# Differential-attention row sums as two rounded products, and a regrouped output turn, in a four-layer trunk on one core

## The reference, cut to what matters

```
q, k, v = split(h @ w_in, 3)
q = rmsnorm(q.reshape(b, s, 8, 2, 64), g_qk[0])     # mean of squares over 64 columns
k = rmsnorm(k.reshape(b, s, 8, 2, 64), g_qk[1])
q, k = rope(q), rope(k)                              # latent tokens only
o = attention(q[..0], k[..0], v) - lam * attention(q[..1], k[..1], v)
out = rmsnorm(o, g_sub) * (1 - lambda_init) @ w_o
```

## Time and profile before

| | |
|---|---|
| median of 3 runs | 3439.49 us (3432.17 to 3446.27) |
| profiled execution | 3442.12 us, its span 3440.3 us |
| mean granted TensorE clock | 0.981 of full |
| PE busy | 3282.2 us (95%) |
| PEld busy | 3025.7 us (88%) |
| DVE busy | 2004.8 us (58%) |
| ACT busy | 1120.1 us (33%) |
| HBM traffic over the span | 88 GB/s |

### The profile page before, as it was taken

One profiled execution on the slowest core, in us unless ns is written; L12 is line 12 of the kernel. 1 busy time (PEld: TensorE's weight loads), 2 busy tenths in 40 slices (PEclk: granted clock), 3 DMA queues, 4 the chain that ended last, 5 costly groups with the idle time before them and its releaser, 6 DMA issues.

```text
span 3440.3 us, 53088 instructions
## 1 busy us (share of the span) xinstructions
PE 3282.2 (95%) x20608; PEld 3025.7 (88%) x20608; DVE 2004.8 (58%) x3059; ACT 1120.1 (33%) x1800; POOL 64.8 (2%) x48
## 2 busy tenths in 40 slices
PE   7899999999999998999999898999999988999999
PEld 4776689999997775999999876899999888999999
DVE  4333357777476665766854754676763888633333
ACT  3244433111145554411112444331111486311111
POOL 1211000000000000000000000000000000000000
PEclk9999999999999998999999999999999999999999
DMA  5111124455221110244532200144542221222222
GB/s 193 56 51 41 40 68 147 156 167 160 72 77 44 44 37 17 68 166 147 171 104 66 69 20 17 57 147 145 174 120 67 74 61 49 74 74 73 73 73 79
DMA packets 436802, 304.29 MB, mean 88 GB/s; under 512 B 12483, under 2 KB 414534, under 8 KB 435654
## 3 DMA queue, kind: packets, MB, share of 16 engines
q1 hardware_dynamic: 426340, 293.75, 28.2%
q10 hardware_dynamic: 10338, 8.88, 0.8%
HBM read 298.49 MB, written 4.10 MB: 88 GB/s over the span
## 4 chain that ended last, share of the span: by engine, by line
PE 85%; DVE 8%; ACT 3%; DVEq 1%; issue 1%; DMA 1%; ACTq 0%; SPq 0%
PE psA L351 29%; PE psB L351 29%; PE psD L351 7%; PE psC L414 3%; PE psA L395 3%; PE psC L367 2%; PE psB L395 2%; PE psC L406 2%; DVE work L2348 1%; PE psB L952 1%; PE psD L893 1%; PE psA L952 1%; DVE act_lo L2356 1%; DVE work L2673 1%; PE psD L925 1%
## 5 line engine op out<-in xcount | busy, mean ns | idle before, releaser
L1643 ACT ACTIVATE w_hi<-raw 128x1024 fp32r<-128x1024 f32 (+1 forms) x314 | 324.8, 1035 | 1089.8 <-PE psB L351 731.6
L2239 DVE TENSOR_TENSOR w_lo<-raw,w_hi 128x1024 fp32r<-128x1024 f32 (+1 forms) x315 | 375.8, 1194 | 314.4 <-ACT w_hi L1643 314.1
L351 PE MATMUL psA<-act_hi,w_hi 128*128 128x320 f32 x1536 | 355.7, 313 | 14.2 <-DVE w_lo L2239 14.2
L351 PE MATMUL psA<-act_hi,w_lo 128*128 128x320 f32 x1536 | 356.1, 314 | 0.0
L351 PE MATMUL psB<-act_hi,w_lo 128*128 128x320 f32 x1536 | 354.5, 312 | 0.0
L351 PE MATMUL psA<-act_lo,w_hi 128*128 128x320 f32 x1536 | 353.2, 311 | 0.0
L351 PE MATMUL psB<-act_hi,w_hi 128*128 128x320 f32 x1536 | 351.4, 310 | 0.0
L351 PE MATMUL psB<-act_lo,w_hi 128*128 128x320 f32 x1536 | 351.1, 310 | 0.0
L2269 DVE SCALAR_TENSOR_TENSOR work<-work,silu_c 128x1024 f32<-128x1024 f32 x266 | 330.0, 1282 | 12.6 <-issue 0.4
L351 PEld LDWEIGHTS psA<-act_hi,w_hi 128*128 128x128 f32 x1536 | 261.7, 191 | 16.5 <-issue 16.2
L351 PEld LDWEIGHTS psB<-act_hi,w_hi 128*128 128x128 f32 x1536 | 260.7, 189 | 0.0
(11 more groups left out here) (360 smaller groups left out, 5619.2 us busy)
## 6 DMA issues: line engine op xcount, KB each, us to landing
raw<-in_w_ffn_in SPq DMA_DIRECT2D x176, 512.0 KB, 3.8
work<-in_w_mod SPq DMA_DIRECT2D x152, 512.0 KB, 4.4
raw<-in_w_ffn_out SPq DMA_DIRECT2D x64, 512.0 KB, 4.2
raw<-in_w_ffn_out SPq DMA_DIRECT2D x32, 384.0 KB, 3.4
raw<-in_diff_w_in SPq DMA_DIRECT2D x24, 512.0 KB, 3.8
work<-in_w_mod SPq DMA_DIRECT2D x8, 1024.0 KB, 7.1
raw<-in_lru_w_in SPq DMA_DIRECT2D x16, 512.0 KB, 4.2
raw<-in_w_mod SPq DMA_DIRECT2D x12, 512.0 KB, 4.2
```

Source lines behind the costliest of these rows:

```text
L351: last = nc.tensor.matmul(out[:, b, 0:half], w[slot][:, kt * cols + c0:kt * cols + c0 + P], r[:, o:o + half], start=(kt == 0 and p == 0), ...
L1643: nc.scalar.activation(w_hi[s][:, 0:n], raw[s][:, 0:n], ACT.Copy).then_inc(hi_done, 1)
L2239: nc.vector.tensor_tensor(w_lo[s_][:, 0:n], raw[s_][:, 0:n], w_hi[s_][:, 0:n].bitcast(F32), ALU.subtract).then_inc(split_done, 1)
```

## The change

1. In differential heads, ScalarE writes the squares rounded (fp32r) into `s_hi`. VectorE then multiplies the copied query or key with itself in f32 and subtracts `s_hi`, which gives `s_lo`; both are new steps, `sqq` and `sqk`. The row sums become two products per half with a rounded block matrix, of `s_hi` and of `s_lo`. `ssq` waits for `sqq`, `ssk` for `sqk`. In VectorE's order `q_squares` stands ahead of the maximum of tile 3, `k_squares` behind `q_roped`. `s_hi` and `s_lo` are shared by query and key.
2. The output blocks are turned into psC, psD, psA, psB, psC. Six of eight tiles of the first two blocks are turned ahead of the last panel of `out3.2`, the seventh behind that panel, the eighth after the last tile. ScalarE copies and stores blocks 0, 2 and 4; VectorE copies blocks 1 and 3, and SyncE stores them.
3. `WORK` shrinks from 13312 to 13204 columns and `blocks_r` is added, filled by one VectorE copy at the start of layer 1. Some names that nothing uses are defined (left out here).

```diff
+        blocks_r = sb("blocks_r", P, F32R)[:, :]
...
-                       ["evq", "rsq", ... "v"], ["q", "qroped", "k", "kroped"])
+                       ["evq", "rsq", ... "v"], ["sqq", "q", "qroped", "sqk", "k", "kroped"])
...
+        Y_TILES = [psC, psD, psA, psB, psC]
...
+        def square_low(x_, hi, lo, tmp):
+            nc.vector.tensor_tensor(tmp, x_, x_, ALU.mult)
+            nc.vector.drain()
+            return nc.vector.tensor_tensor(lo, tmp, hi.bitcast(F32), ALU.subtract)
...
+        s_hi, s_lo = y_hi[:, 0:T], y_lo[:, 0:T]
...
# SyncE, at its end
+            for t in range(1, QT, 2):
+                sp.wait_ge(y_copied_odd, t // 2 + 1)
+                sp.dma_start(a["y_sample"][0, (t - 1) * P:t * P, :], y_tok[:, t * D:(t + 1) * D]).then_inc(y_out, 16)
...
# TensorE
+            def early_outputs():
+                for t in range(2):
+                    output_turned(t, 0, KT - 2)
...
                         pe.wait_ge(x_done, i * 2 + (base + j - 1))
+                        if j == 1 and between and isinstance(i, int):
+                            between()
...
                     def ssq(h):
-                        acts.wait(pe, "evq", h)
-                        pes.mark(sum_rows(psC, blocks, [dsq_q], TH), "ssq")
+                        dves.wait(pe, "sqq", h)
+                        pes.mark(sum_rows(psC, blocks_r, [s_hi, s_lo], TH), "ssq")
...
                     def ssk(h):
-                        acts.wait(pe, "evk", h)
-                        dves.wait(pe, "qroped", h)
-                        pes.mark(sum_rows(psC, blocks, [dsq_k], TH), "ssk")
+                        dves.wait(pe, "sqk", h)
+                        pes.mark(sum_rows(psC, blocks_r, [s_hi, s_lo], TH), "ssk")
...
+            pe.wait_ge(x_done, x_tiles[0] - 1)
+            for t in range(2):
+                output_turned(t, KT - 2, KT - 1)
             pe.wait_ge(x_done, x_tiles[0])
-            for t in range(QT):
-                if t >= 2:
-                    pe.wait_ge(y_copied, t - 1)
...
+            for t in range(2):
+                output_turned(t, KT - 1, KT).then_inc(y_turned, 1)
+            for t in range(2, QT):
+                if t == 4:
+                    pe.wait_ge(y_copied, 1)
+                output_turned(t, 0, KT).then_inc(y_turned, 1)
...
# ScalarE
-                        acts.mark(evacuate(dq_t[h.k % 2], dsq_q, psD, TH), "evq")
+                        acts.mark(evacuate(dq_t[h.k % 2], s_hi, psD, TH), "evq")
...
-            for t in range(QT):
+            for t in range(0, QT, 2):
...
# VectorE
+                    nc.vector.tensor_copy(blocks_r, blocks)
...
                         probs(h, 2)
+                        prep(q_squares)
                         largest(h, 3)
...
                         prep(q_roped)
+                        prep(k_squares)
                         largest(h, 4)
...
# VectorE, first head: q_squares at step 2 of the norm's loop, k_squares at step 7
...
+            for t in range(1, QT, 2):
+                dve.wait_ge(y_turned, t + 1)
+                nc.vector.tensor_copy(y_tok[:, t * D:(t + 1) * D].rearrange("p (b n) -> p b n", b=2),
+                                      Y_TILES[t][:, :, :]).then_inc(y_copied_odd, 1)
```

More of the change, by code:

```diff
@@ L41 @@
 SLOT = 8 * P
-WORK = 13312
+WORK = 13204
 MUNIT = 1024
@@ L293, in build @@
         y_turned, y_copied, y_out = sem("y_turned"), sem("y_copied"), sem("y_out")
+        y_copied_odd = sem("y_copied_odd")
         def steps(name, pe, act, dve, base=1):
@@ L544, in build @@
         mV = [c(6 * P), c(6 * P)]
+        sq_at = CKV_AT + 2 * NKEY
+        n_hi, n_lo = (t_[:, sq_at:sq_at + T] for t_ in (h_hi, h_lo))
+        k_hi, k_lo = (t_[:, sq_at:sq_at + NKEY] for t_ in (h_hi, h_lo))
+        r_hi, r_lo = (t_[:, sq_at + NKEY:sq_at + NKEY + T] for t_ in (h_hi, h_lo))
         m_probs = [[c(T)], [c(T)]]
@@ L974, in _, with output_turned, project @@
             x_tiles = [KT]
-            def project(name, kts, rows, last_source, plan=None, place=None, paired=False):
+            def output_turned(t, k0, k1):
+                for kt in range(k0, k1):
+                    last = nc.tensor.transpose(Y_TILES[t][:, kt // 4, (kt % 4) * P:(kt % 4 + 1) * P],
+                                               x[:, kt * T + t * P:kt * T + (t + 1) * P], ident)
+                return last
+            def early_outputs():
+                for t in range(2):
+                    output_turned(t, 0, KT - 2)
+            def project(name, kts, rows, last_source, plan=None, place=None, paired=False, between=None):
                 base = x_tiles[0]
@@ L998, in project @@
                                 last.then_inc(gemm_done, 1)
-                turns_and_mods(turn, 1 if paired else 0, KT // 2, plan, place)
+                turns_and_mods(turn, 1 if paired else 0, KT // 2 - (1 if between else 0), plan, place)
+                if between:
+                    turn(KT // 2 - 1)
                 x_tiles[0] += KT
@@ L1510, in _ @@
                     project(f"out{layer}.{ch}", size, (h_hi, h_lo), lambda: pe.wait_ge(hidden_done, base + size + 1),
-                            modulation_of(layer), ("out", ch))
-            pe.wait_ge(x_done, x_tiles[0])
-            for t in range(QT):
-                if t >= 2:
-                    pe.wait_ge(y_copied, t - 1)
[L1518 to L1522, removed]
+                            modulation_of(layer), ("out", ch),
+                            between=early_outputs if (layer, ch) == (DEPTH - 1, len(FFN_CHUNKS) - 1) else None)
+            pe.wait_ge(x_done, x_tiles[0] - 1)
+            for t in range(2):
+                output_turned(t, KT - 2, KT - 1)
+            pe.wait_ge(x_done, x_tiles[0])
+            for t in range(2):
[4 more added lines that the diff above has]
+                output_turned(t, 0, KT).then_inc(y_turned, 1)
         @block.scalar
@@ L1905, in first_query @@
                     def first_query():
-                        acts.mark(taken(2, 0, dq_t[0], dsq_q), "evq")
+                        acts.mark(taken(2, 0, dq_t[0], s_hi), "evq")
                     def first_key():
-                        acts.mark(taken(2, 1, dk_t[0][:, 0:T], dsq_k), "evk")
+                        acts.mark(taken(2, 1, dk_t[0][:, 0:T], s_hi), "evk")
                     norm(2, {0: first_query, 1: lambda: high(Head(0, 1), 0), 2: lambda: rsq(h0), 3: lambda: cached(h0),
@@ L2124, in _ @@
                     x_tiles[0] += KT
-            for t in range(QT):
+            for t in range(0, QT, 2):
                 act.wait_ge(y_turned, t + 1)
                 nc.scalar.activation(y_tok[:, t * D:(t + 1) * D].rearrange("p (b n) -> p b n", b=2),
-                                     psum[t % 2][:, :, :], ACT.Copy).then_inc(y_copied, 1)
-                act.wait_ge(y_copied, t + 1)
+                                     Y_TILES[t][:, :, :], ACT.Copy).then_inc(y_copied, 1)
+                act.wait_ge(y_copied, t // 2 + 1)
                 dst = a["y_prompt"][0] if t == 0 else a["y_sample"][0, (t - 1) * P:t * P, :]
@@ L2512, in _, with q_squares, k_squares @@
                     scale = 64 ** -0.5
+                    dve.wait_ge(const_in, 16)
+                    nc.vector.tensor_copy(blocks_r, blocks)
+                    def q_squares(h):
+                        acts.wait(dve, "evq", h)
+                        dves.mark(square_low(dq_t[h.k % 2], s_hi, s_lo, dsq_q), "sqq")
+                    def k_squares(h):
+                        acts.wait(dve, "evk", h)
+                        dves.mark(square_low(dk_t[h.k % 2][:, 0:T], s_hi, s_lo, dsq_k), "sqk")
                     def q_normed(h):
@@ L2575, in _ @@
                     h0 = Head(0, 0)
-                    norm(2, {1: lambda: rescale(2, 0, psD, first + 1, dq_t[0]), 3: lambda: low(Head(0, 1), 0),
+                    norm(2, {1: lambda: rescale(2, 0, psD, first + 1, dq_t[0]), 2: lambda: q_squares(h0), 3: lambda: low(Head(0, 1), 0),
                              4: lambda: rescale(2, 1, psA, first + 2, dk_t[0][:, 0:T]), 5: lambda: q_normed(h0),
-                             6: lambda: q_roped(h0), 8: lambda: k_normed(h0)})
+                             6: lambda: q_roped(h0), 7: lambda: k_squares(h0), 8: lambda: k_normed(h0)})
                     rescale(2, 2, psB, first + 3, dvt)
```

5 lines of the change are left out of this document (3 added, 2 removed).

## The result

| | before | after |
|---|---|---|
| median (6 executions of each) | 3439.32 us | 3459.41 us (3456.83 to 3464.7) |
| ratio, 95% interval | | 1.0058 [1.0048, 1.0068] |
| profiled execution, its span | 3442.12, 3440.3 us | 3464.7, 3462.9 us |
| mean granted TensorE clock | 0.981 | 0.976 |

The change made the kernel 20.1 us slower by the medians. The prediction said 3454 us, with 3445 to 3465 as its range. Page of the kernel after: busy time and instructions by engine, then the engines' shares of the chain that ended last, the answer to the earlier trace rows.

The account below looks back on a forecast made before the run. It took TensorE's stream plus its standstills to bound the kernel. Query -2.5, key +9.2, first head +3.7, clock +4.8 and output -0.2 gave +15.0 us; from the median 3454.5, predicted 3454 us, range 3445 to 3465.

Parts of the forecast that it names:

- rival 1: Differential heads: the clock falls in nearly every head, all seven at 1.7 to 3 us; +24, 3464 us; chance 0.17.
- Cheaper sums: Row sums on TensorE: four fp32r instructions take 0.59 us instead of 1.08, saving 0.49 us per sum, 16 sums.
- Rival 4: Row sums: the f32 sums don't get cheaper by rounding; 7.8 us more, 3462; chance 0.04.
- Query, heads 2 to 8: Query's sums: squares hidden with about 0.03 us wait, except 0.75 in the second head; sum -2.5 us.
- Key, heads 2 to 8: Key's sums: squares not hidden, TensorE stands still 2.2 us; +1.3 per head, +9.2 us for 7 heads.
- Rival 3: Key's sums: the wait is absorbed or never arises and the change gains; -10, 3430 us; chance 0.04.
- First head: First differential head: squares delay VectorE's norm, TensorE waits 3.6 us at `rotq`, about 3 at `ssk`; +3.7 us.
- Output: Output turn at the end: first store 0.6 us later, stores 6.45 instead of 7.3 us at 406 GB/s; -0.2 us.
- Clock: Differential heads: stalls lower TensorE's clock, 3 falls of 7 at 1.6 us; +4.8 us, between 0 and 21.

Follow-up runs that it names:

- e2: Kernel before plus the new output turn and only the query's sums as two rounded products, key's sums plain f32: 3444.91 us, ratio 1.0011.
- e4: Full change plus 14 unused fp32r products per head keeping TensorE busy through the stall before the key's sums: 3452.25 us, ratio 1.0035 to the kernel before.
- e5: Full change with turned tile 3 and part of the value's products moved ahead of the key's sums: 3453.93 us, ratio 1.0048 to the kernel before.
- e9: Kernel before plus new output turn and two rounded products only for query's sums from the third head on: 3438.82 us, ratio 0.9994.
- e3: Kernel before plus the new output turn and only the key's sums as two rounded products, query's sums plain f32: 3462.94 us, ratio 1.0064.
- e8: Full change with the old output turn: 3464.44 us, ratio 1.0079 to the kernel before.
- e10: Full change with the key's squares ahead of the rotated query on VectorE: 3466.03 us, ratio 1.0071 to the kernel before.
- e1: Kernel before plus the new output turn alone, all differential-head sums plain f32: 3437.67 us, ratio 0.9992.

## Why the prediction was right, and which term was too small

The time lies in the range, and the mechanism and its place were the forecast's. The number is less of a hit: +20.1 lies halfway between the forecast's +15 and rival 1's +24, six falls are more than the one to five that the forecast spanned, and the range holds the result because it was drawn to take in most of rival 1. By its steps:

- **Cheaper sums** held to the digit at full clock: 0.59 us for four, saved 0.49 each. Rival 4 is out. Behind a fall the key's sums take about twice that.
- **Query, heads 2 to 8** (−2.5) held: waits of 0.71 and six times none. e2's windows show −0.4 a head.
- **Key, heads 2 to 8** (+9.2) held: a wait of 2.29 where 2.2 was said. With the clock kept up (e4) the six windows grew by 5.11 us, 0.85 a head; the working gives 1.3 − 0.49 + 0.03 = 0.84. Rival 3 is out: nothing absorbed the wait, even where I tried to provide cover (e5).
- **First head** (+3.7) held: VectorE's `k_normed` comes 22.96 us behind the marker instead of 19.28, +3.7. Up to the second head's rotation it is +4.1 in the kernel after and in e4 alike, with 0.26 of it the second head's query; how near that lies is in part luck, since in this stretch e9, with e1's work, is 1.5 us shorter by its clock alone. The second stall was shorter than I said (1.24, not 3 us): behind the 3.46 us stall TensorE ran on the lowered clock (0.63 and 0.52 in the four microseconds from 1024) and came later itself. In e3, which has no such first stall, it is 2.79. The one hid in the other, as the step had it.
- **Output** (−0.2): 0.0. The cost of the early turns was 1.3 (1.4 said), and the stores followed each other more closely: the 2.62 MB took 7.0 us at 375 GB/s in the mean, against 7.3 at 358 in the earlier trace rows. I had taken a best slice, 406, for the mean, and 6.45 us.
- **Clock** (+4.8): this is the term that was mis-sized. I took three falls of seven at 1.6 us. The price of one was nearly right (1.4 by e4's windows), the count was not: six heads of seven fell, 458.35 − 448.8 = 9.5 us in layer 1 by e4, of which 1.1 lies behind the seventh head's key. The excess of 4.7 us over the term is all of the 4.6 by which layer 1 (+19.8) exceeds its part of the sum (15.2); without the clock it grew by 10.3, where the sum has 10.4.

The profiled execution lies 5.3 us over its kernel's median, so the medians are the fairer comparison: +20.1 measured, +15.0 said. The number of falls is rival 1's, its price per fall (1.9) and its extra microsecond in the first head are not; its 3464 lies about as far above the median (4.6) as the forecast lies below (5.4). I had read the count from layer 2, where three of seven heads with 2.31 us of standing still lost the clock. That time came in two pieces there, 1.36 and 0.94 us with 0.77 us of work between, and the key's wait is one piece of 2.29. e5 fits this reading: up to 3.06 us in a head, in pieces of at most 1.31 with 3 to 5 us between, and no fall in six. One piece of 2.29 was followed by a fall in six heads of seven in the kernel after and in e3 and in all seven in e8, one of 2.51 to 2.92 in all seven of e10. It is no fixed rule: the wait of 2.79 us in e3's first head had no fall behind it.

The Trainium skill, page "TensorE: Matmul & The Clock Gate", section "A second HAM failure mode: psum-queue depth-cycling", tells of short idle stretches between matmul groups, frequent enough to make the clock oscillate. The traces agree that idle stretches can make the clock move between its two levels, here with one stall of 2.29 us in some 45 and a fall behind six of seven. By the count of e5 it is not frequency alone, since three shorter stalls in a head brought no fall.

The Trainium skill, page "DMA: Bandwidth & Descriptors", section "Specifications", gives about 358 GB/s as a core's limit to HBM. The trace differs: 375 GB/s over the 7.0 us of the stores, 418 in one slice, so the measurement decides, and it is no cap on these stores.

**Open:** why e2's median is 7 us over e1's, and why e9's 3.5 us don't show in its median. Executions of one kernel scatter by more than either, and the scatter goes with the clock: of the 27 executions of the kernel before that ran beside e1 and e2, the shortest (3430.6 us) has a mean clock of 0.984 and the longest (3447.89) 0.979, and e8's layer 2 shows how falls that come or stay away make 6 us. Whether e2 draws more falls for a reason or by chance is not shown. Nor is why the head at 1071.74 kept its clock with the same stall as the others (in e3 too, while in e8 and e10 it fell), or why e3's first head did.

## What to carry to other kernels

Before moving work off a saturated engine, look at the chain that feeds it, not at the helper's mean load: VectorE was 58% busy and could still not take 1.73 us, because they stood between its last operation and TensorE's next. Price a stall twice, once for itself and once for the clock behind it, and count one long piece for more than several short ones of the same sum that lie well apart (e5 against the kernel after). If a stall can't be removed, idle products put into it give back the clock's share (9.5 of 19.8 us here), which also is the cleanest way to measure that share.

## What was not expected of the hardware

A single stall of 2.29 us, with TensorE otherwise over 90% busy, was followed by a fall from 2.4 to 1.2 GHz in six of seven heads, at about 1.4 us each; 14 products of no use in its place prevented every one. The fall comes when TensorE is at work again, so it shows as longer busy time and not as waiting. The chain of waits alone would have put it down to TensorE. And the falls are not the same in every execution: in layer 2, on equal code, they made one stage 275.7 us in one execution and 281.5 to 281.9 in eleven others.
